# Projection stage: whole float32 products in one pass against split float32 products in four passes

## The reference, cut to what matters

```
hn = rms_norm(x, attn_norm_g)
z = hn @ w_in                       # 1024 -> 6 x 512: q | k | v | zr | zk | zv
q = apply_rope(rms_norm(q), cos, sin); k likewise   # 16 groups of 64
dh = token_shift(hn) - hn
w: (tanh((hn + dh*mu0) @ w1)) @ w2 + w0;  a: ((hn + dh*mu1) @ a1) @ a2 + a0 ; g: sigmoid((hn + dh*mu2) @ g1) @ g2
```

## Time and profile before

| | us |
|---|---|
| median of 3 runs | 3841.83 (3839.81 to 3844.22) |
| profiled execution, device time | 3845.27 |
| its span, first to last instruction | 3843.7 |
| TensorE busy | 3398.9 (88%) |
| VectorE busy | 1318.6 (34%) |
| ScalarE busy | 937.3 (24%) |
| GpSimd busy | 854.9 (22%) |
| the big product of the stage, L372, busy | 664.5 |

### The profile page before, as it was taken

One profiled execution on the slowest core, in us unless ns is written; L12 is line 12 of the kernel. 1 busy time (PEld: TensorE's weight loads), 2 busy tenths in 40 slices (PEclk: granted clock), 3 DMA queues, 4 the chain that ended last, 5 costly groups with the idle time before them and its releaser, 6 DMA issues. The chain is left out here.

```text
span 3843.7 us, 68767 instructions
## 1 busy us (share of the span) xinstructions
PE 3398.9 (88%) x25568; PEld 2160.4 (56%) x25569; DVE 1318.6 (34%) x2377; ACT 937.3 (24%) x2006; POOL 854.9 (22%) x1064
## 2 busy tenths in 40 slices
PE   4999999998889857778888599589999999999699
PEld 2554545454566636777777588434444444444487
DVE  1222222223677743444444333611111111111455
ACT  1111111112677743333333211000000000000232
POOL 1000000000214146666666100000000000000343
PEclk9999999999999978999899899689999999999799
DMA  5111111113200021111111366545775955763343
GB/s 185 58 60 38 57 55 60 49 41 112 75 8 15 7 80 63 69 58 58 58 58 36 102 214 212 191 155 201 265 274 196 335 210 194 299 245 147 135 154 110
DMA packets 221713, 474.74 MB, mean 124 GB/s; under 512 B 26897, under 2 KB 62865, under 8 KB 221489
## 3 DMA queue, kind: packets, MB, share of 16 engines
q1 hardware_dynamic: 200864, 404.30, 29.8%
q0 software_dynamic: 11552, 41.95, 3.1%
q10 hardware_dynamic: 9072, 25.17, 1.6%
HBM read 358.65 MB, written 112.73 MB: 123 GB/s over the span
## 5 line engine op out<-in xcount | busy, mean ns | idle before, releaser
L372 PE MATMUL p_z<-w_in_sb,hnT 128*128 128x512 f32 x1536 | 664.5, 592 | 0.0
L372 PEld LDWEIGHTS p_z<-w_in_sb,hnT 128*128 128x128 f32 x1536 | 290.6, 190 | 353.9 <-issue 352.0
L2093 PE MATMUL pe_gate<-w_gate_sb,e_xT 128*128 x752 | 334.4, 598 | 7.2 <-issue 6.2
L2103 PE MATMUL pe_y<-w_down_sb,e_hT 128*128 x752 | 330.6, 592 | 1.2 <-DVE e_hT L2036 1.2
L2093 PE MATMUL pe_up<-w_up_sb,e_xT 128*128 x752 | 330.4, 592 | 0.0
L2093 PEld LDWEIGHTS pe_up<-w_up_sb,e_xT 128*128 128x128 f32 x752 | 142.9, 190 | 179.8 <-issue 179.8
L2053 DVE TENSOR_TENSOR e_h<-e_silu,pe_up 128x512 f32<-128x512 f32 x47 | 32.3, 688 | 611.7 <-issue 475.0
L2093 PEld LDWEIGHTS pe_gate<-w_gate_sb,e_xT 128*128 128x128 f32 x752 | 140.4, 192 | 168.2 <-issue 168.1
L2103 PEld LDWEIGHTS pe_y<-w_down_sb,e_hT 128*128 128x128 f32 x752 | 139.2, 190 | 158.8 <-issue 158.8
L1981 POOL COPY e_idx<-row_tokens 128x1 uint32 (+1 forms) x48 | 8.7, 182 | 962.3 <-PE pe_xT L2066 903.3
L1447 PE MATMUL pd_out<-d_w_out_part,d_mixT 128*128 128x512 f32 x768 | 189.0, 402 | 11.7 <-DVE d_w_out_part L1440 11.7
(11 more groups left out here) (397 smaller groups left out, 5385.1 us busy)
## 6 DMA issues: line engine op xcount, KB each, us to landing
w_gate_sb<-in_w_gate_dram SPq DMA_DIRECT2D x32, 2048.0 KB, 10.6
w_up_sb<-in_w_up_dram SPq DMA_DIRECT2D x32, 2048.0 KB, 15.6
w_down_sb<-in_w_down_dram SPq DMA_DIRECT2D x32, 2048.0 KB, 20.3
s_y<-e_y ACTq DMA_DIRECT2D x47, 512.0 KB, 8.2
s_y<-d_zeros SPq DMA_DIRECT2D x16, 1024.0 KB, 6.5
w_in_sb<-in_w_in_dram SPq DMA_DIRECT2D x6, 2048.0 KB, 19.8
s_zr<-z_stage SPq DMA_DIRECT2D x48, 256.0 KB, 2.0
s_lora<-z_stage SPq DMA_DIRECT2D x48, 256.0 KB, 2.1
```

What stands on the lines that cost most here:

```text
L372: last = nc.tensor.matmul(pZ[:, c % 3, :], hT[s][:, k, 1:P + 1], w_sb[:, k, c * BANK:(c + 1) * BANK], start=(k == 0), stop=(k == KD - 1))
L2093: last = nc.tensor.matmul(bank[:], xT[:, k, :], w[:, bass.ds(slot, 1), k, :].rearrange("p o n -> p (o n)"), start=(k == 0), stop=(k == KD ...
L2103: last = nc.tensor.matmul(p_y[:, half, :], hT[:, k, :], wd[:, bass.ds(slot, 1), k, half * BANK:(half + 1) * BANK].rearrange("p o n -> p (o ...
```

## The change

The projection is made with split float32 products. W_in no longer fits as both parts at once, so the tokens are passed four times: pass 0 makes zr and all of the LoRA, pass 1 q and k, pass 2 v, pass 3 zk and zv (`W_PASSES`). `w2` holds three chunks of W_in, each as a high and a low part; a chunk is loaded in four pieces into tiles that are idle at the time (`landing`), split by ScalarE and VectorE between tiles, and put where a used chunk lay (`W_SLOT`). The transposed, normalised tile is split once, in pass 0, into `hn_split` (high and low, 1 MB), stored to a new DRAM tensor `s_hT`, and read back three times, once for each later pass, into three buffers. `p_z` has four banks. The order of z results is written out in the list `order`, and every engine's program is straight code, without the loop over pairs. SP's queue starts with x, the gain and the first chunk of W_in; positions come last. The q and k gains are loaded once and broadcast. In q and k's normalisation the scale is applied last, so that the rotation does not wait for it. q and k of a tile and their rotated forms lie in the space of the LoRA weights, which pass 0 has used up.

```diff
+F32R = mybir.dt.float32r
+PARTS = ((0, 0), (0, 1), (1, 0))
+W_PASSES = ((3,), (0, 1), (2,), (4, 5))
+W_ORDER = (3, 0, 1, 2, 4, 5)
+W_SLOT = (1, 2, 0, 0, 1, 2)
...
+            def load_h(m):
+                i = m % TILES
+                sp.wait_ge(z_done, read_until(m - 3))
+                if m - 3 < TILES:
+                    sp.wait_ge(stash[m % 3], 16 * ((m - 3) // 3 + 1))
+                sp.wait_ge(stash[i % 3], 16 * (i // 3 + 1))
+                sp.dma_start(hs[m % 3][:].rearrange("p a k n -> p (a k n)"), t["hT"][i * P:(i + 1) * P, :]).then_inc(h_in[m % 3], 16)
...
+            load_x(0)
+            sp.dma_start(gain[:], t["attn_norm_g"].partition_broadcast(P)).then_inc(s_gain, 16)
+            for n in range(W_PIECES):
+                load_w(n)
...
+            for i in range(TILES):
+                load_h(TILES + i + 2)
+                if i >= 1:
+                    store_qk(i - 1)
+                if 9 <= i < 9 + W_PIECES:
+                    load_w(4 * W_PIECES + i - 9)
+            for i in range(TILES):
+                load_h(2 * TILES + i + 2)
+                store(("v", i))
+                if 5 <= i < 5 + W_PIECES:
+                    load_w(5 * W_PIECES + i - 5)
+                if i == 0:
+                    store_qk(TILES - 1)
...
+            def high(i):
+                act.wait_ge(hTa, i + 1)
+                act.wait_ge(hTd, i + 1)
...
+                nc.scalar.copy(hs[i % 3][:, 0, :, :].bitcast(F32R), hT[i % 2][:, :, 1:P + 1]).then_inc(h_high, 1)
...
+            def low(i):
+                dve.wait_ge(h_high, i + 1)
+                part = lambda k: hs[i % 3][:, k, :, :].bitcast(F32R)
+                nc.vector.tensor_tensor(part(1), hT[i % 2][:, :, 1:P + 1], part(0), ALU.subtract).then_inc(h_low, 1)
...
+                dve.wait_ge(sq_done, i + 1)
+                nc.vector.tensor_reduce(qss[:], qsq[:], AX.X, ALU.add).then_inc(qss_done, 1)
+                dve.drain()
+                nc.vector.tensor_tensor(q3[:, :, 0:h], by_cos[:, :, 0:h], by_sin[:, :, h:DH], ALU.subtract)
+                nc.vector.tensor_tensor(q3[:, :, h:DH], by_cos[:, :, h:DH], by_sin[:, :, 0:h], ALU.add)
+                if i >= 1:
+                    k_turned(i - 1)
+                dve.drain()
+                dve.wait_ge(qrs_done, i + 1)
+                nc.vector.tensor_tensor(q3, q3, qrs[:].unsqueeze(2).broadcast_to([P, 16, DH]), ALU.mult).then_inc(rot_done, 1)
...
-                    for k in range(KD):
-                        last = nc.tensor.matmul(pZ[:, c % 3, :], hT[s][:, k, 1:P + 1], w_sb[:, k, c * BANK:(c + 1) * BANK],
-                                                start=(k == 0), stop=(k == KD - 1))
...
+                    for a, b in PARTS:
+                        last = nc.tensor.matmul(bank, hs[m % 3][:, a, k, :].bitcast(F32R), w_part(c, b)[:, k, :].bitcast(F32R),
+                                                start=(k == 0 and a == b == 0), stop=(k == KD - 1 and a == 1))
...
+            for p in range(1, 4):
+                for i in range(TILES):
+                    m = p * TILES + i
+                    pe.wait_ge(h_in[m % 3], 16 * len(range(TILES + (m - TILES) % 3, m + 1, 3)))
+                    for name, c in zip(NAMES[p], W_PASSES[p]):
+                        chunk(p, i, name, c)
+                    if p == 1 and i >= 1:
+                        turn_qk(i - 1)
+                    if p == 2 and i == 0:
+                        turn_qk(TILES - 1)
```

More of the change, by code:

```diff
@@ L104, in phase_project, with w_part, piece, pieces_after @@
         block = ctx.enter_context(nc.Block())
+        def w_part(c, k):
+            return w2[W_SLOT[c]][k]
+        def piece(n):
+            return W_ORDER[n // W_PIECES], slice((n % W_PIECES) * KP, (n % W_PIECES + 1) * KP)
+        def pieces_after(p, i):
+            for pass_, tile, first in ((0, 5, 4), (0, 10, 8), (1, 4, 12), (2, 1, 16), (2, 9, 20)):
+                if p == pass_ and tile <= i < tile + W_PIECES:
+                    return [first + i - tile]
+            return []
+        def landing(n):
+            room = (qsq, by_cos, by_sin, qkT) if n < 3 * W_PIECES else (x_sb[0], x_sb[1], hT[0], hT[1])
+            room = room[n % W_PIECES][:]
+            flat = room if len(room.shape) == 2 else room.rearrange("p a b -> p (a b)")
+            return flat[:, 0:KP * BANK].rearrange("p (k n) -> p k n", k=KP)
@@ new lines, in _ @@
+            act.wait_ge(s_zero, 1)
+            square(0)
+            raw(0)
+            high(0)
+            for n in range(W_PIECES):
+                split(n)
+            for i in range(TILES):
+                if i + 1 < TILES:
+                    square(i + 1)
+                lora_mid(i)
+                if i + 1 < TILES:
+                    raw(i + 1)
+                    high(i + 1)
+                if i >= 1:
+                    lora_out(i - 1)
+                for n in pieces_after(0, i):
+                    split(n)
+                if i == 2:
+                    act.wait_ge(s_const, 1)
+                    act.wait_ge(s_ang, 1)
+                    nc.scalar.activation(sin_t[:], ang, ACT.Sin)
+                    act.wait_ge(s_ang, 2)
+                    nc.scalar.activation(cos_t[:], turns, ACT.Sin, bias=half_pi[:], scale=-1.0).then_inc(s_trig, 1)
@@ new lines, in _ @@
+            low(0)
+            for n in range(W_PIECES):
+                split(n)
+            mix_lora()
+            for i in range(TILES):
+                if i + 1 < TILES:
+                    make_hn(i + 1)
+                if i == 0:
+                    evac(("zr", 0))
+                if i + 1 < TILES:
+                    raw(i + 1)
+                    low(i + 1)
+                if i >= 1:
+                    evac(("zr", i))
+                l1_turned(i)
+                if i == 0:
+                    dve.wait_ge(s_out, 6 * 16)
+                if i >= 1:
+                    evac(("w", i - 1))
+                    evac(("a", i - 1))
+                for n in pieces_after(0, i):
+                    split(n)
+                if i == 1:
+                    angles()
@@ new lines, in _ @@
+            chunk(0, 0, "zr", 3)
+            pe.wait_ge(s_wl_rdy, 1)
+            lora_in(0)
+            transposes(1)
+            turn_l1(0)
+            pe.wait_ge(s_out, 6 * 16)
+            for i in range(1, TILES):
+                lora_in(i)
+                if i + 1 < TILES:
+                    transposes(i + 1)
+                pe.wait_ge(h_low, i + 1)
+                chunk(0, i, "zr", 3)
+                turn_l1(i)
+                lora_out(i - 1)
+            lora_out(TILES - 1)
```

572 lines of the change are left out of this document (317 added, 255 removed).

## The result

| | us |
|---|---|
| median before, in the comparison with the change | 3843.02 (3839.81 to 3846.48) |
| median after, 4 runs | 3677.53 (3677.04 to 3678.79) |
| ratio | 0.957, 95% interval 0.9553 to 0.9586 |
| profiled execution after, span | 3675.3 |

A forecast was written before the change was run, and what follows sets the result against it. TensorE alone was taken to bound the projection stage. Terms -115.8 - 12 - 5.7 + 2 + 3 + 4 = -124.5 us took the profiled 3845.27 to 3720.8; with the median 3.4 lower, forecast 3717.5 us, range 3706 to 3740.

The forecast's parts named there:

- The product: Projection stage: each of 96 chunks goes from 6.87 to 5.66 us, -115.8 us, all of it on the path.
- Rival 6: Projection: split product takes exactly half a whole float32 instruction, 0.215 us, 5.15 per chunk, total 3669 us; chance 0.02.
- The first tile: Start: first zr chunk runs while TensorE waits, -5.7 us; first tile's LoRA middle, no longer covered, +2.
- Seams: Reload wait between passes 0 and 1, +3 us (1 to 6); rotated q/k wait before pass 2, +4 (2 to 7).
- Reloads: Split tiles read back in passes 1 to 3 arrive in time: price 0, bounds 0 and +25 us.
- splitting: Splitting tiles and weights on ScalarE and VectorE is covered, price 0; otherwise about 1 us in each of 8 tiles.
- q/k pass: With a weight piece VectorE is busy 12.0 of 12.3 us per tile; it fits narrowly, price 0.
- Rivals 2, 3, 4 and 5: Reloads bind v pass, +25, 0.06; VectorE binds q/k, +28, 0.03; reloads in all passes, 3960, 0.02; split products slow, 4160, 0.01.
- The start: First LoRA input product starts near 46 us instead of 57.65: -12, bounds -18 and +1; positions priced at about 10.
- Rival 1: The start is not earlier, as queue order also depends on SP's issuing of elements: +12, 3730 us; chance 0.12.
- What follows the stage is unchanged in work: Stages after the projection: work unchanged, so 0 us difference predicted.
- written-out programs: Straight code replacing loops over two tiles: nothing won, as TensorE shows no idle time at the loop's seams.

The follow-up runs named there:

- a_seam: Changed kernel with the first two split-tile reloads of pass 1 queued earlier and the last q/k transposes behind the second v chunk: 3666.2 us.
- b_gain: Kernel before, with the q and k gains loaded in 2 copies instead of 16 and broadcast: 3822.8 us, ratio 0.995.
- b_pos: Kernel before, with the positions' DMA moved behind the LoRA weights and biases on SP's queue: 3851.7 us, ratio 1.002.
- b_posgain: Kernel before, with the positions moved behind the LoRA weights and 2 gain copies instead of 16: 3830.9 us, ratio 0.9973.
- b_pad101: Kernel before, with 101 empty TensorE instructions ahead of its first transposes, moving the recurrent loop from 141 to 242 of 256: 3820.5 us, ratio 0.9942.
- a_pad155: Changed kernel with 155 empty TensorE instructions ahead of its first transposes, putting the recurrent loop at 141 and expert loop at 16 of 256: 3699.1 us.
- b_long: Kernel before, with 4709 empty TensorE instructions ahead of its first transposes, putting both loops at the changed kernel's instruction numbers: 4128.2 us, expert stage 1057.8.
- a_seam_e16: a_seam with 155 empty TensorE instructions at the head of the output stage, moving only the expert loop from 117 to 16 of 256: 3662.7 us.

## Why the prediction was wrong

The direction was right, and so was that TensorE alone bounds the stage. Three things failed: the price list of the start (13.4 us), the size of the product (the larger part of 12.6) and the step from unchanged work to unchanged time (17.9). Step by step:

- **The product**, 96 x (6.87 - 5.66): mis-sized. In the q/k pass the tile took 11.79 us where I had 12.25 (-7.4 in 16 tiles), in the 48 chunks of the last two passes 5.44 where I had 5.66 (-10.5); in pass 0 my 17.9 per tile was right (17.81). The rows I used mixed a start stamp right behind its load with one 0.23 us behind. Rival 6 (0.215 us per matmul) had the right direction: 0.227 was measured, about half way from my 0.236.
- **The first tile**: its zr chunk did run in waiting time (21.80), as said, and the wait for the first LoRA middle was 1.15 us where I had 2.
- **Seams**: 4.0 and 4.8 us for 3 and 4, inside their bounds. Not counted was the clock behind them, about 4 us (a_seam). With the product this makes -7.4 - 10.5 + 1.8 + 4, about -12, of the -12.6 by which the projection fell short of my figure.
- **Reloads, splitting, q/k pass**: nothing, as said. The DMA share was 0.76 in the v pass, 1 MB landed in 5.1 us where I took 5.0, and TensorE has less than 0.5 us of idle time in the windows of the passes. Rivals 2, 3, 4 and 5 are out.
- **The start**: -12 against -25.4, below my bound of -18. The step that failed: I priced the positions at 10 us of the queue, the whole time until they landed, and the gain copies on ScalarE's queue at nothing, without a row for them. b_gain shows the gain copies at 22.8 us, and the landings in b_pos and b_posgain show the positions at about 1. Rival 1 fell as well.
- **"What follows the stage is unchanged in work"**: true, and no reason for unchanged time. This step failed and is the largest part. The recurrent stage gave 27.7 us by where its loop begins (b_pad101, a_pad155); the expert stage took 11.0, by all that the runs show by where its loop lies (b_long). I said of the written-out programs that nothing is won; that step looked at the projection only.

Against the forecast: start -13.4, projection -12.6, later stages -17.9, together -43.9 us in the profiled spans (-40.0 in the medians). The later stages could as well have gone the other way: with the loop at 141, as in a_pad155, the same change would have taken 3699 us. That part of the gain is luck of placement.

The kernel with mended seams and its expert loop moved (a_seam_e16) takes 3662.7 us, ratio to the kernel before 0.9518 (0.9502 to 0.9534), 15 us under the changed kernel.

## What to carry to other kernels

Read the pace of a repeated product between stamps inside its run, or over many repetitions, not from its start to that of the next kind. Ask of every DMA of small rows which transfers run at the same time on other queues, before pricing the one that is waited for. When a change lengthens a program in front of a loop, the time of that loop can move by a per cent or two either way though its code is the same. Some empty instructions in waiting time test it. Time the stages apart from each other before crediting a total to an edit.

## What the hardware showed

- R differs by 28 us (2.3%) with the recurrent loop of TensorE at 141 or 242 of 256 instructions, in both directions and in kernels of both families. That a branch costs a fetch agrees with the 3.4 to 4.3 us in front of the loop's first matmul. The same section of the Trainium skill calls the crossing of a block mostly hidden. In the iterations shown above the jump gives at most 1 us of the 5.7 us of difference. Of the rest about 2 us are other "issue" waits in the body (7.1 and 5.1 us) and 3 are waits for ScalarE's `c_X` (5.4 and 2.4 us). Why these depend on the place is not shown.
- A split product in a long run takes 227 ns per matmul of 512 columns at full granted clock.
- 14 more DMAs of 128 rows of 256 bytes on ScalarE's queue stretched three element-wise DMAs on SP's from 7.29 to 19.96 us of issue, and let the LoRA weights behind them land 22.7 us later.
- During waits of 4 and 4.8 us the granted clock fell to its lower level, and it stayed there for some 4 to 5 us of work behind them; without the waits it did not fall (a_seam).
